# Gate and up of a ConvFFN as 2 by 2 blocks with seven block products, and the down product after all 44 blocks

## What is computed

```python
D_MODEL = 2048; D_FF = 5632; CONV_W = 3; D_PLE = 256
def conv_ffn(h, buf, w_gate, w_up, conv_w, conv_b, w_down):
    L = h.shape[1]
    g = h @ w_gate
    ext = jnp.concatenate([buf.astype(g.dtype), g], axis=1)
    c = conv_b
    for j in range(CONV_W):
        c = c + ext[:, j:j + L] * conv_w[j]
    out = (jax.nn.silu(c) * (h @ w_up)) @ w_down
    return out, ext[:, L:]
...
    x = x + jnp.concatenate([o_att, o_rnn], axis=-1) @ w_out
    ffn, conv_buf = conv_ffn(rms_norm(x, norm_ffn), conv_buf0, w_gate, w_up, conv_w, conv_b, w_down)
    x = x + ffn
    x = x + jax.nn.sigmoid(rms_norm(x, norm_ple) @ w_ple_gate) * (p[i] @ w_ple_proj)
```

## Time and profile before

| | us |
|---|---|
| median of 3 runs (2798.0 to 2798.22) | 2798.04 |
| the profiled execution, its own time | 2796.97 |
| its span (first to last instruction) | 2795.2 |
| PE busy | 2766.3 (99%) |
| PE weight loads busy | 2560.2 (92%) |
| DVE busy | 1546.1 (55%) |
| ACT busy | 1027.3 (37%) |
| DMA, mean rate | 106 GB/s |
| stage "ffn", about 1048 to 2572 | 1524 |

### The profile page before, as it was taken

How to read it: one execution, slowest core, us unless ns; L and a number is a source line. 1 busy time by engine, 2 the same in 40 slices (tenths; PEclk the granted TensorE clock), 3 DMA queues, 4 the chain that set the end, 5 groups by cost and what they waited for, 6 DMA issues and landing times.

```text
span 2795.2 us, 53116 instructions
## 1 busy us (share of the span) xinstructions
PE 2766.3 (99%) x20175; PEld 2560.2 (92%) x20175; DVE 1546.1 (55%) x2683; ACT 1027.3 (37%) x1453; POOL 0.8 (0%) x7
## 2 busy tenths in 40 slices
PE   7999999999999999999999999999999999999998
PEld 7989889889889999999999999999999999999998
DVE  5666666666576465545544455444455445565444
ACT  6445545545544243222322223322233222244322
POOL 0000000000000000000000000000000000000000
PEclk9999999999999999999999999999999999999999
DMA  6344343344446333332333323333323333233332
GB/s 218 106 140 116 97 140 115 107 131 116 117 127 207 102 91 90 90 90 86 92 100 92 90 85 89 98 90 91 94 83 91 97 93 90 83 93 92 107 106 85
DMA packets 549184, 295.59 MB, mean 106 GB/s; under 512 B 16040, under 2 KB 539170, under 8 KB 549066
## 3 DMA queue, kind: packets, MB, share of 16 engines
q1 hardware_dynamic: 516762, 268.49, 32.9%
q10 hardware_dynamic: 32320, 25.68, 2.9%
HBM read 272.63 MB, written 21.66 MB: 105 GB/s over the span
## 4 chain that ended last, share of the span: by engine, by line
PE 93%; DVE 3%; ACT 2%; issue 1%; DMA 0%; SPq 0%; ACTq 0%; DVEq 0%
PE product L944 28%; PE product L948 15%; PE product L945 15%; PE product L946 15%; PE product L947 14%; PE scratch L730 2%; PE scratch L738 1%; DVE w_lo L1535 1%; ACT score L1126 1%; ACT w_hi L1115 1%; PE scratch L814 1%; DVE s_state L1686 1%; PE scratch L777 1%; PE scratch L830 0%; ACT sqx L1126 0%
## 5 line engine op out<-in xcount | busy, mean ns | idle before, releaser
L944 PE MATMUL product<-act,w_hi 128*128 128x512 f32 x2816 | 1134.5, 403 | 4.7 <-DVE act L1814 4.6
L1115 ACT ACTIVATE w_hi<-w_raw 128x1024 fp32r<-128x1024 f32 (+1 forms) x496 | 514.9, 1038 | 1020.6 <-PE product L948 965.4
L1535 DVE TENSOR_TENSOR w_lo<-w_raw,w_hi 128x1024 fp32r<-128x1024 f32 (+1 forms) x496 | 593.4, 1196 | 524.4 <-ACT w_hi L1115 524.1
L948 PE MATMUL product<-act,w_lo 128*128 128x264 f32 x2816 | 805.3, 286 | 0.0
L946 PE MATMUL product<-act,w_hi 128*128 128x264 f32 x2816 | 800.4, 284 | 0.0
L945 PE MATMUL product<-act,w_hi 128*128 128x264 f32 x2816 | 797.9, 283 | 0.0
L947 PE MATMUL product<-act,w_lo 128*128 128x256 f32 x2816 | 788.8, 280 | 0.0
L946 PEld LDWEIGHTS product<-act,w_hi 128*128 128x128 f32 x2816 | 527.9, 187 | 122.2
L944 PEld LDWEIGHTS product<-act,w_hi 128*128 128x128 f32 x2816 | 532.9, 189 | 22.3 <-issue 18.0
L945 PEld LDWEIGHTS product<-act,w_hi 128*128 128x128 f32 x2816 | 534.9, 190 | 1.0
L948 PEld LDWEIGHTS product<-act,w_lo 128*128 128x128 f32 x2816 | 530.2, 188 | 0.0
(11 more groups left out here) (261 smaller groups left out, 2231.6 us busy)
## 6 DMA issues: line engine op xcount, KB each, us to landing
w_raw<-in_w_in SPq DMA_DIRECT2D x112, 512.0 KB, 3.8
w_raw<-in_w_gate SPq DMA_DIRECT2D x88, 512.0 KB, 3.7
w_raw<-in_w_up SPq DMA_DIRECT2D x88, 512.0 KB, 3.7
w_raw<-in_w_down SPq DMA_DIRECT2D x64, 384.0 KB, 3.3
w_raw<-in_w_down SPq DMA_DIRECT2D x64, 320.0 KB, 3.1
w_raw<-in_w_out SPq DMA_DIRECT2D x32, 512.0 KB, 4.0
w_raw<-in_w_ple_gate SPq DMA_DIRECT2D x32, 384.0 KB, 3.3
k_pages<-in_cache_k SPq DMA_DIRECT2D x128, 64.0 KB, 2.6
```

The source lines that it names most:

```text
L944: pe.matmul(both, hi, x[:, k, 0:2 * TA], start=begin, stop=False)
L948: mm = pe.matmul(far, lo, x[:, k, 2 * TA:TA + T], start=False, stop=end)
L1115: act.activation(w_hi[:, slot, 0:n, :], w_raw[:, slot, 0:n, :], ACT.Copy).then_inc(w_hi_ready, 1)
L1535: dve.tensor_tensor(flat(w_lo[:, slot, 0:n, :]), flat(w_raw[:, slot, 0:n, :]), flat(w_hi[:, slot, 0:n, :]).bitcast(F32), ALU.subtract).the ...
```

## The change

**Gate and up as one 2 by 2 product.** The 16 feature tiles are two halves (tiles 0 to 7, 8 to 15), the 520 tokens are two halves of 260 ("near", "far"), and the outputs are gate and up. These are eight block products. The new kernel makes seven, from sums and differences of the four input blocks (`x_sums_of`, made once) and of the four weight blocks (`w_difference`, four per block of 128 FFN features). Each block product is 8 k-steps of three matmuls of 260 columns. The products add up in three PSUM regions, X, Y and Z: X starts with product 0, takes 2, 4 and 6; Y takes 1; Z takes 3 and 5. ACT copies X after 0 and after 2, and Z after 3, to SBUF. DVE combines: near gate = Y + copy, far up = X + copy, near up = Z + copy, far gate = X.

**Weights.** Each of the seven weight sets is split by ACT and DVE (128x1024 each) and lies in a ring of four slots: product j uses slot 0, 1, 2, 3, 0, 1, 2. Gate chunks are loaded into `w_raw`, up chunks into `w_more`.

**Through DRAM.** `x_sets` holds four input sets, `x_late` the other three in the room of `act2`, beside half of the weight ring. Gate, taps, silu, up and u take the room of `xT`. So the residual tiles are written to `x_scratch` as they are made, two of the sums go through `sums_scratch`, and each block's u (128 x 520) is written to `u_scratch`. The residual comes back in two lots of eight tiles: 8 to 15 in the last blocks, 0 to 7 in the third output tile of the down product.

**Down.** All 44 blocks run first, then the four down groups of 16 x 11 k-steps. The 11 u tiles of a group are read back through a ring of four buffers and split. Up is not scaled by `R` any more, the down product is (`scaled`, `ffz`). The loading and turning of p moves into the down product. The FFN is written out, not looped.

```diff
+RING_SLOT = (0, 1, 2, 3, 0, 1, 2)
+SLOT_BEFORE = (3, 3, 3, 7, 4, 4, 4)
...
+        def load_gate(f, i):
+            sp.wait_ge(w_lo_ready, prep(f - 1, (3, 6)[i]) + 1)
+            sp.dma_start(raw_gate[i], w_gate[:, i * KC:(i + 1) * KC, f * P:(f + 1) * P]).then_inc(w_landed[i], 16)
+        def load_up(f, i):
+            if f > 0:
+                sp.wait_ge(w_lo_ready, prep(f - 1, (4, 5)[i]) + 1)
+            sp.dma_start(raw_up[i], w_up[:, i * KC:(i + 1) * KC, f * P:(f + 1) * P]).then_inc(flag(f"up_in{i}"), 16)
+        def u_load(n):
+            if n >= U_RING:
+                sp.wait_ge(flag("u_lo_done"), n - U_RING + 1)
+            sp.wait_ge(flag("u_stored"), (n + 1) * 16)
+            sp.dma_start(u_raw[:, n % U_RING, :], u_d[n]).then_inc(flag(f"u_in{n % U_RING}"), 16)
...
+                for f in range(FB):
+                    X = X_BANK[f % 2]
...
+                    product(f, 0, X, True)
...
+                        pe.wait_ge(flag("combined"), C11 + STEPS_C * (f - 1))
+                    product(f, 1, Y_BANK, True)
...
+                    pe.wait_ge(flag("copied"), copy_step(f, 0))
+                    product(f, 2, X, False)
...
+                        pe.wait_ge(flag("combined"), C12 + STEPS_C * (f - 1))
+                    product(f, 3, Z_BANK, True)
+                    pe.wait_ge(flag("copied"), copy_step(f, 1))
+                    product(f, 4, X, False)
+                    pe.wait_ge(flag("copied"), copy_step(f, 2))
+                    product(f, 5, Z_BANK, False)
+                    pe.wait_ge(flag("combined"), C22 + STEPS_C * f)
+                    product(f, 6, X, False)
...
+        def first_tap(f):
+            act.wait_ge(flag("combined"), GATE_A + STEPS_C * f)
+            act.wait_ge(flag("combined"), C21 + STEPS_C * f)
+            func(ffc, ffg[:, 2:T + 2], ACT.Identity, scale=vec(COL_CW[2] + f), bias=vec(COL_CW[3] + f)).then_inc(flag("copied"), 1)
...
+                    copy_of(f, 0, X_BANK[f % 2], p1_copy, C11)
+                    w_part(f, 4)
...
+                    w_part(f, 5)
+                    if f > 0:
+                        first_tap(f - 1)
+                    copy_of(f, 2, X_BANK[f % 2], u2_copy, C12)
+                    if f > 0:
+                        silu(f - 1)
...
+                    copy_of(f, 3, Z_BANK, p5_copy, C22)
...
+                    w_part(f, 6)
...
+            elif what == "down":
+                for g in range(GROUPS):
+                    for n in range(KT):
+                        if g == 0 and n == 2:
+                            sp.wait_ge(flag("u_stored"), FB * 16)
...
+                            for k in range(KC):
+                                sp.dma_start(xT[:, k, :], xt_d[k]).then_inc(flag(f"tile_in{k}"), 16)
+                            sp.wait_ge(flag("conv_out"), 16 + GROUPS * 2 * 16)
```

More of the change, by code:

```diff
@@ L179 @@
 EARLY_MIXED = 4
+BACK_AFTER = [1 if k in MIX_DIRECT else 2 for k in range(KT)]
 PAD_AT = 26
@@ L238, in program @@
     ctx = ExitStack()
-    early, heads, late = ExitStack(), ExitStack(), ExitStack()
+    acts, early, heads, late = ExitStack(), ExitStack(), ExitStack(), ExitStack()
     def sem(name):
@@ L387, in program @@
[L387 to L396, removed]
+    x_sets = lt("x_sets", [P, KC, 2, EARLY_SETS * TH], F32R)
@@ L1340, in write_x, with x_in_columns @@
             act.dma_start(xt_d.rearrange("k p t -> p k t")[:, :, t0:t1], xT0[:, :, t0:t1]).then_inc(flag("xT_written"), 16)
+        def x_in_columns(it, apart=False):
+            k = it - 1
+            act.wait_ge(flag("x_made"), k * 5)
+            if apart or not isinstance(it, int):
+                act.wait_ge(flag("late_out"), k * 16)
+            for x in range(2):
+                act.wait_ge(g_free[x], it + g_rnn[x])
+                func(x_cols[:, x:x + 6:5, :], column(xT, k + x * KC).rearrange("p (h t) -> p h t", h=2), ACT.Copy,
+                     scale=gain_of("norm_ffn", k + x * KC)).then_inc(flag("x_part"), 1)
@@ L1414, in out_product @@
                     act.wait_ge(g_free[x], it + (g_rnn[x] + 1))
-                    squares(it * 2 + (SUM_EARLY + x), x, column(xT, it * 2 + x))
-                with act.Fori(0, KT // 4) as it:
-                    for x in range(2):
-                        out_product(it, x)
-                b = take("p_turn", 0)
-                func(pT[:, :, 0:SEQ], M[b][:, :, :], ACT.Copy).then_inc(free[b], 1)
-                b = take("ps_turn", 0)
-                func(pT[:, :, SEQ:T], M[b][:, 0, 0:2 * NS].rearrange("p (a c) -> p a c", a=2), ACT.Copy).then_inc(free[b], 1)
@@ L1423, in visit @@
[L1423 to L1437 removed]
+                    squares(it * 2 + (SUM_EARLY + x), x, column(xT, it + x * KC))
@@ new lines, in x_sums_of @@
+        def x_sums_of(it, apart=False):
+            step = flag("x_made")
+            n = it * 5 - (4 if apart else 5)
+            a11, a12, s2, s1, s3, a21, a22 = [x_cols[:, i, :] for i in range(7)]
+            s4 = a21
+            dve.wait_ge(flag("x_part"), it * 3 - 1)
+            dve.tensor_tensor(s1, a22, a21, ALU.add).then_inc(step, 1)
+            dve.tensor_tensor(s3, a11, a21, ALU.subtract).then_inc(step, 1)
+            dve.wait_ge(step, n + 1)
+            dve.tensor_tensor(s2, s1, a11, ALU.subtract).then_inc(step, 1)
+            dve.wait_ge(step, n + 3)
+            dve.tensor_tensor(s4, a12, s2, ALU.subtract).then_inc(step, 1)
@@ L1920, in visit @@
[L1920 to L1926 removed]
+                for x in range(2):
+                    out_product(0, x)
@@ L1927, in visit @@
+                with dve.Fori(1, KT // 2 - 1) as it:
+                    out_product(it, 0)
+                    x_sums_of(it)
+                    out_product(it, 1)
+                    x_lows(it)
+                it = KT // 2 - 1
+                out_product(it, 0)
+                x_sums_of(it)
+                w_difference(0, 1)
+                w_difference(0, 2)
+                out_product(it, 1)
+                x_lows(it)
                 pad(0)
-                for k in range(KC, KT):
-                    operand_of("norm_ffn", k, 2 * KT + k + 1)
```

768 lines of the change are left out of this document (529 added, 239 removed).

## The result

| | before | after |
|---|---|---|
| median, us | 2798.02 (2797.66 to 2798.22, 4 runs) | 2773.41 (2771.13 to 2775.9, 4 runs) |
| span of the profiled execution | 2795.2 | 2772.5 |
| PE, DVE, ACT busy | 2766.3, 1546.1, 1027.3 | 2670.9, 1859.3, 1212.6 |

The ratio is 0.9913, interval 0.9901 to 0.9925: faster by 25 us or 0.9%, where 94 us were forecast. The time lies 69 us above the forecast and 15 us above its range. PE lost 95 us of work and gained about 73 us of idle time.

What follows compares the result with a forecast made beforehand. PE's matmuls bound the kernel. Profiled 2796.97 - 126 (columns) + 16 (stage start) + 10.6 (passage to down) + 5 (third output tile) = 2702.6 us; the median shown is 1.1 higher, so 2704, range of 8 in 10 2682 to 2758.

Steps and rivals of the forecast that it cites:

- the down product costed at nothing: Down stage: u writes and scaling, about 5 us of DVE under 7.9 of PE, lie beside PE and add 0.
- each DVE microsecond over a product shows 64 times: Down stage: if the cover of PE's work is gone, each DVE microsecond over a product counts 64 times.
- Columns: Gate and up blocks: 43680 columns instead of 49920, 22.89 us becomes 20.03, saving 44 x 2.86 = 126 us.
- DVE in a block: Gate and up blocks: DVE needs 16.9 us of 20.0 and keeps up; tightest is product 5, with 0.95 us to spare.
- rivals 1 and 2: Blocks: the first has DVE's chain later than counted, product 5 waiting about 1 us, 2747 us, 15%; the second is rival 2.
- rival 2: Blocks: the gate chunk loop bounds if landings exceed about 5.5 us; 9.2 makes it as slow as before; 5%.
- Start of the stage: Block 0 of gate and up: late input sets, sums through DRAM and `conv_in` add 16 us, bounds 8 and 24.
- T0: The end of the last "out" product, from which times at the start of the gate and up stage are counted.
- Out stage: Residual writes lie beside PE and are costed at nothing.
- From the blocks to down, and the third tile: Head of the down product: +10.6 us; third output tile, weights behind eight residual tiles and p: +5, bounds 0 and 9.
- T1: The end of the last block's product 6, from which times at the head of the down product are counted.
- Written-out code: Writing the FFN out adds no price: the heads are written out already, their PE busy 748 of 754 us.

Runs made afterwards that it cites:

- e1: In the down product of the changed kernel, ACT copies the next group's u tile before the second weight chunk: 2734.09 us.
- e2: In the down product of the changed kernel, DVE's low of the next group's u tile moves behind scaling, the second chunk's low and the addition: 2734.5 us.
- e3: Changed kernel with the eleven loads of `conv_in` issued early, in the out stage behind the first up chunks: 2764.52 us.
- e5: Changed kernel with each pair of weight loads in the out stage issued ahead of the previous pair of residual writes: 2762.4 us.

## Why the prediction was wrong, step by step

**The step that failed: the down product costed at nothing.** The prediction put the work under it "beside PE and costed at nothing", because about 5 us of DVE fit under 7.9 us of PE. The sum of work was right (5.0 us of DVE in the tile of 9.00 shown above) and the conclusion was not. I followed one *block* instruction by instruction through ACT's and DVE's orders, and did not do so for one *output tile*, whose order had changed as well: u tile preparation had been inserted between a wait and the chunk that PE needs next. The price is 36 us by rows and 39 by e1 and e2, of the 69 by which the forecast missed. My warning "each DVE microsecond over a product shows 64 times" had the multiplier in mind and the wrong cause: it is not time over a product, but a place in the queue, and it shows in 32 tiles. Followed in the same way, the tile would have given it: product end + 0.2, copy 1.0, u high 0.6, u low 0.7, scaling 1.4, low 1.2 = 5.1 us against 4.3.

**Columns.** Right in kind, 6 us off in size. A block takes 1142.68 - 1122.41 = 20.27 us against 22.99; 44 x 2.72 = 120 us instead of 126. Seven eighths of the columns give 20.03 and the turn 0.1; the rest, 0.14, is spread over 168 matmuls. If a matmul costs a price per column and one for itself, the two blocks (49920 columns in 160 matmuls in 22.87 us, 43680 in 168 in 20.15) give about 5 ns for itself. The timeline does not bear that out. Averaged over the 257 k-steps of the kernel before from 1100 to 1290 that have no turn beside them, a matmul of 512 columns takes 0.233 us from start to start and one of 256 takes 0.117, just half, where 5 ns would make it 0.231 and 0.118. Those of 264 columns take 0.120 to 0.123 by their place in the k-step, those of 260 take 0.120 in the changed kernel. So a price per matmul is not shown, and why 260 columns take nearly 1 ns more than seven eighths would give stays open. The Trainium skill (TensorE: Matmul & The Clock Gate, Back-to-back issue gap) has 2.5 ns for each; with its figures the gain came out at 113 us. The measured 120 lies in the middle, and the page's absolute time was off, as the prediction said.

**DVE in a block, rivals 1 and 2.** Right: PE has no gap of note in 43 blocks, DVE is at 82% (85 forecast). ACT waited for gate chunks in every block but one, since they took 4.7 us to land (3.7 in the earlier trace rows):

```profile
ACT w_hi L1703 <- DMA w_raw<-in_w_gate: 162.1, 43, 5.8
```

```profile
w_raw<-in_w_gate SPq DMA_DIRECT2D x88, 512.0 KB, 4.7
```

PE waited once for a weight set in these blocks, 0.72 us, so the slack held. With 162 us of waits it looks like a bound in a list by size, and is none. The prediction had named this wait as the sign of rival 2; it appeared and the rival did not come true, so the sign was ill chosen. Rival 2's prices do not follow from its loop either: with 14 us beside the landing, a landing of 9.2 makes a block of 23.2 us, 3.2 above 20.03, and 43 of these are 137 us, about 2841 and not the time of before.

**Start of the stage: 16 forecast, 27 measured.** The mechanism was as told, the sizes were too small. PE's timeline of block 0:

```profile
1061.25 0.59 PE L1185 MATMUL product<-x_sets,w_hi 128*128 128x260 f32 x1 [6.29 <-DVE x_sets L2149]
1064.83 0.59 PE L1185 MATMUL product<-x_sets,w_hi 128*128 128x260 f32 x1 [2.57 <-DVE x_sets L2149]
...
1080.17 1.04 PE L1211 MATMUL scratch<-const,conv_in 16*128 16x16 f32 x8 [8.31 <-DMA conv_in<-in_state_ffn_conv]
...
1099.04 0.39 PE L1185 MATMUL product<-act 128*128 128x260 f32 x1 [2.27 <-DVE xT L2306]
```

They are 19.4 us of idle time (16 forecast). The rest, 7.7 us, is mostly clock: its mean in that stretch is 0.77, and behind the second of these waits matmuls of 260 columns start 0.22 us apart. I added nothing for it there, although had shown half-clock k-steps after an idle stretch. `conv_in` came at T0 + 27.6 instead of 21. Its last issue is later since the sums went to DRAM only at 1066.29, and each of the eleven takes 0.42 us on SP and more, where I had 0.316. With e3 and e5 together the block ends at T0 + 38.7 (45.1 less 0.3 for the turn and the 6.1 by which the far gate stands in block 1); the forecast was 38.5. That is partly luck: PE's idle time in that block is 11.8 us (16 forecast), and the clock, which the forecast left out, makes up for it.

**Out stage: 0 forecast, about 4 measured.** I costed the residual writes by their DMA time and not by what waits behind them in SP's queue. PE waited four times for a chunk, some 13 us apart, 0.74 to 1.28 us and 4.0 in all; the first:

```profile
1002.58 0.50 PE L1095 MATMUL product<-act,w_hi 128*128 128x512 f32 x1 [1.08 <-DVE w_lo L1828]
```

e5 removes them.

**From the blocks to down, and the third tile.** 10.6 and 5 were forecast. The first tile ended at T1 + 22.7 instead of 18.5, behind 8.55 us of idle time (7.9 forecast), slow k-steps (1.44, 1.30 and 1.19 us) and further waits for u tiles. The second tile's first chunk was then another 1.4 late. The third tile's was 4.79 late, with some 2.5 us of slow k-steps behind it. Together about 8 us more. The turning of p in this stage, 1.5 us, stood in no term.

**Written-out code: 0 forecast.** At 852.57, in a head stage that the edit left alone, PE has an idle time that nothing releases:

```profile
847.75 2.39 PE L965 MATMUL scratch<-wT,v_nat 128*128 128x128 f32 x20
852.57 0.77 PE L1095 MATMUL product<-act,w_hi 128*128 128x512 f32 x1 [2.43 <-issue]
```

At the same place before, the product begins 2.2 us behind the start of the turns (848.92 and 846.74), here 4.8. PE's list of waits has no such entry for the kernel before, and one of 2.0 to 2.6 us for the changed kernel and each of the ten edited ones. With 1 us by which the stage is late already at 847.75 (not explained) and the out stage it makes nearly all of the 8.3 of the first stretch. It may be code loading for the longer program; that was not tried and stays open.

**The chances.** 93% stood on faster, which came true. The range failed: its upper end took in a wait of 1 us at one place of the *block*, times 43. It held no case for a wait of 1 us at one place of the *output tile*, times 32.

## What to carry to other kernels

When a change touches the order of instructions in a second loop, follow that loop too, one iteration, on every in-order queue: an instruction that waits for the end of a product should have behind it only what is needed after it, and preparation for later belongs into the engine's idle time ahead of such a wait. An engine at 57% can still make PE late by a microsecond in every iteration; the sign is a small idle time before the same line in most iterations, and the cure is an order, not less work. Do the same for the DMA-issuing queue: a store that waits for its data holds up every load behind it.

## What the runs showed of the hardware

An idle time costs PE more than the list of waits says, in two sizes. Behind the 8.55 us at the head of the down product matmuls of 264 columns start 0.22 us apart, where a full stretch has 0.12, the lower clock level:

```profile
1988.39 0.77 PE L1095 MATMUL product<-x_sets,w_hi 128*128 128x512 f32 x1 [8.55 <-DVE x_sets L2163]
1988.96 0.42 PE L1096 MATMUL product<-x_sets,w_hi 128*128 128x264 f32 x1
1989.18 0.42 PE L1097 MATMUL product<-x_sets,w_hi 128*128 128x264 f32 x1
```

Behind 0.85 us only the first matmul is longer:

```profile
2096.30 0.28 PE L1096 MATMUL product<-x_sets,w_hi 128*128 128x264 f32 x1
```

It starts at 2095.95, so its 512 columns take 0.35 us instead of 0.24. The matmul before it starts at 2094.81 and is recorded as 0.28 us long, where the next one usually starts 0.12 behind it, so another 0.16 us are lost that do not count as idle. That makes 1.13 us for an idle time of 0.85, a third more, in each of the 32 tiles. And eleven small DMA issues that took 0.316 us each on SP before took 0.42 to 1.32 here:

```profile
L776 SPq DMA_DIRECT2D conv_in<-in_state_ffn_conv x44: 416/420/1320, 1070.1 to 1552.0; - x44
```
